# A hybrid mLSTM, attention and expert layer on one core: attention and routing moved into the expert loop

## What is computed

```python
h = modulate(rmsnorm(x, n1), sh1, sc1)
mq, mk, mv, mo, gt, aq, ak, av = split_cols(h @ w_in)
q = rmsnorm(aq.reshape(B, T, A_HEADS, A_DH), qg)          # 8 heads of 64, 2 key groups
m_out = mlstm_mixer(mq, mk, mv, mo, gt, ...)              # 4 heads of 128, both directions
a_out = attn_latent(rope_2d(q), rope_2d(k), v, kc, vc, sink)   # window of +-128 and 128 cached keys
x = x + g1 * (concat([m_out, a_out]) @ w_out)
h2 = modulate(rmsnorm(x, n2), sh2, sc2)

def peer(h, w_q, sub_a, sub_b, u_tab, v_tab):
    q = (x @ w_q).reshape(N, P_HEADS, P_DKEY)             # 8 heads, 2 halves of 128
    va, ia = lax.top_k(sa, 16); vb, ib = lax.top_k(sb, 16)    # sa, sb: q halves against 128 keys
    cand = va[..., :, None] + vb[..., None, :]
    top, pos = lax.top_k(cand, 16)                        # 8 x 16 = 128 experts per token
    gates = softmax(top)
    a = gelu(einsum('pd,phkd->phk', xb, u_tab[eb]))
    return einsum('phk,phkd->pd', gb * a, v_tab[eb])
x = x + g2 * peer(h2, ...)
```

## Time and profile before

| what | value |
|---|---|
| three runs, us | 4431.73, 6284.15, 4428.21 |
| median, us | 4431.73 |
| the profiled execution, us | 4423.65 |
| its span in the profile, us | 4421.8 |
| TensorE, busy share | 67% |
| VectorE, busy share | 54% |
| ScalarE, busy share | 19% |
| POOL, busy share | 36% |
| moved by DMA | 1348.41 MB, mean 305 GB/s |

### The profile page before, as it was taken

How to read it: one execution, slowest core, us unless ns; L and a number is a source line. 1 busy time by engine, 2 the same in 40 slices (tenths; PEclk the granted TensorE clock), 3 DMA queues, 4 the chain that set the end, 5 groups by cost and what they waited for, 6 DMA issues and landing times.

```text
span 4421.8 us, 41953 instructions
## 1 busy us (share of the span) xinstructions
PE 2957.5 (67%) x11157; PEld 1284.8 (29%) x11157; DVE 2402.1 (54%) x5728; ACT 826.1 (19%) x2523; POOL 1578.3 (36%) x1434
## 2 busy tenths in 40 slices
PE   8899778888863656656656655755755755755555
PEld 1444366555542212212312311311311411411111
DVE  1232354333316774674674684684684684685554
ACT  1111123323311111111111111111111111111111
POOL 0000011101102454454454454454554454455453
PEclk9899887777677878877877877877978977967777
DMA  9101133111134999999999999999999999999998
GB/s 368 56 34 41 59 101 114 39 43 47 38 130 189 418 415 390 420 409 389 420 404 391 420 408 391 420 404 391 416 408 402 409 395 408 409 404 406 403 420 368
DMA packets 220971, 1348.41 MB, mean 305 GB/s; under 512 B 23370, under 2 KB 34250, under 8 KB 71370
## 3 DMA queue, kind: packets, MB, share of 16 engines
q0 software_dynamic: 165888, 1208.03, 67.1%
q1 hardware_dynamic: 47212, 113.48, 7.4%
q10 hardware_dynamic: 7776, 25.96, 1.5%
HBM read 1316.04 MB, written 31.33 MB: 305 GB/s over the span
## 4 chain that ended last, share of the span: by engine, by line
DMA 37%; PE 12%; issue 10%; DVE 7%; POOL 3%; ACT 1%; POOLq 0%; SPq 0%; DVEq 0%; ACTq 0%
DMA pe_ring<-arg_uv,pe_fetch_idx 34%; PE pe_acc L1357 10%; POOL pe_ring L1311 3%; DMA pe_h<-h_scratch 2%; DVE pe_ring L1550 2%; PE pe_qP L1335 2%; ACT pe_diag L1423 1%; DVE pe_w L1555 1%; DMA pe_w_q<-arg_w_q 0%; DVE pe_rest L1514 0%; DVE pe_pos L1480 0%; DVE pe_ab L1517 0%; DVE pe_scores L1492 0%; DVE pe_rest L1511 0%; ACT pe_gelu L1418 0%
## 5 line engine op out<-in xcount | busy, mean ns | idle before, releaser
L1357 PE MATMUL pe_acc<-pe_ring,pe_diag 128*64 128x512 f32 x4608 | 1527.5, 799 | 1220.6 <-ACT pe_diag L1423 1220.6
L1311 POOL DMA_INDIRECT pe_ring<-arg_uv,pe_fetch_idx x1152 | 1391.4, 1208 | 1554.8 <-PE pe_acc L1357 1304.7
L1550 DVE CUSTOM_DVE_ANT_0 pe_ring<-pe_ring,pe_h 128x1024 f32<-128x1024 f32 x1152 | 1405.6, 1225 | 850.0 <-DMA pe_ring<-arg_uv,pe_fetch_idx 777.2
L1357 PEld LDWEIGHTS pe_acc<-pe_ring,pe_diag 128*64 128x64 f32 x4608 | 344.8, 167 | 2294.4 <-ACT pe_diag L1423 1809.4
L1418 ACT ACTIVATE pe_gelu<-pe_dot 128x2 f32<-128x2 f32 x576 | 117.1, 203 | 1876.9 <-DVE pe_dot L1550 1876.8
L1423 ACT ACTIVATE pe_diag<-pe_pick,pe_w 128x64 f32<-128x64 f32 x1152 | 337.9, 340 | 606.0 <-DVE pe_w L1555 606.0
L351 PE MATMUL in_z<-w_in,in_hT 128*128 128x512 f32 (+1 forms) x864 | 356.8, 576 | 22.3 <-ACT in_hT L381 22.3
L1335 PE MATMUL pe_qP<-pe_h2T,pe_w_q 128*128 128x128 f32 x2304 | 298.5, 285 | 29.3 <-DMA pe_w_q<-arg_w_q 29.3
L1335 PEld LDWEIGHTS pe_qP<-pe_h2T,pe_w_q 128*128 128x128 f32 x2304 | 273.8, 196 | 139.4 <-issue 139.4
L351 PEld LDWEIGHTS in_z<-w_in,in_hT 128*128 128x128 f32 x864 | 168.3, 196 | 205.7 <-issue 198.0
L1555 DVE TENSOR_TENSOR pe_w<-pe_gelu,gates 128x2 f32<-128x2 f32 x576 | 92.1, 160 | 189.0 <-ACT pe_gelu L1418 117.9
(11 more groups left out here) (256 smaller groups left out, 2418.4 us busy)
## 6 DMA issues: line engine op xcount, KB each, us to landing
ada_w<-arg_w_ada SPq DMA_DIRECT2D x12, 2048.0 KB, 10.3
pe_ring<-arg_uv,pe_fetch_idx POOLq DMA_INDIRECT x1152, 11.6
w_in<-arg_w_in SPq DMA_DIRECT2D x8, 1416.0 KB, 21.0
ml_qkT<-qkT_scratch SPq DMA_DIRECT2D x18, 512.0 KB, 3.5
pe_h<-h_scratch SPq DMA_DIRECT2D x36, 256.0 KB, 12.7
pe_w_q<-arg_w_q SPq DMA_DIRECT2D x8, 1024.0 KB, 12.9
ada_x<-arg_x ACTq DMA_DIRECT2D x9, 512.0 KB, 6.4
in_xn<-arg_x SPq DMA_DIRECT2D x9, 512.0 KB, 3.8
```

The costliest lines, as they stand in the source:

```text
L1311: pool.indirect_dma_start(out=ring[j][:], out_offset=None, in_=io.uv, in_offset=bass.IndirectOffsetOnAxis(ap=idg[half][:, j:j + 1], axis=0 ...
L1357: mm = pe.matmul(acc[b][cg * TOKS:(cg + 1) * TOKS, :], diag[:, j, :], ring[j][:, D + b * 512:D + (b + 1) * 512], start=False, stop=False)
L1550: dve.tensor_tensor_reduce(out=ring[j][:, 0:D], in0=ring[j][:, 0:D], in1=h2[i % NC][:], scale=1.0, scalar=0.0, op0=ALU.mult, op1=ALU.add, ...
```

## The change

`attend` and `peer` become one block, `mix_and_experts`. Attention (called the mixer) is cut into 19 steps per tile, routing into up to 44. One function, `drive`, lays out the order for every engine: the mixer of tile 0 alone; the routing of tile 0 with the mixers of tiles 1 and 2 beside it; then the expert loop, in which each of the first 128 pairs is followed by one routing step and one mixer step (114 mixer steps are left for them). Everything is written out straight, no loop is left. Scores, transposes and tails share two PSUM banks `ST`, so two heads are now done at a time: scores of both, then exp, transposes and values of both.

The pair itself. The gates no longer go through VectorE after the gelu; a block of eight selection matrices is filled with them ahead, and ScalarE scales it by the gelu:

```diff
-                        act.activation(gelu[:, sl], dot[:, sl], ACT.Gelu_apprx_tanh).then_inc(s_gelu, 1)
-                        act.wait_ge(s_w, n * NB + (q + 1))
-                            act.activation(diag[:, i % GROUP, :], pick[:], ACT.Copy, scale=w[:, i:i + 1]).then_inc(s_diag, 1)
+                    act.wait_ge(s_dot, (n + 1) * NC)
+                    act.activation(gelu[:, sl], dot[:, sl], ACT.Gelu_apprx_tanh).then_inc(s_gelu, 1)
+                    act.wait_ge(s_fill, n * NC // FILL + 1)
+                        last = act.activation(wsel[:, i, :], wsel[:, i, :], ACT.Copy, scale=gelu[:, i:i + 1])
-                        dve.tensor_tensor(w[:, sl], gelu[:, sl], g.gates[...], ALU.mult).then_inc(s_w, 1)
+                    if (r * NC) % FILL == 0:
+                        dve.tensor_tensor(wsel[:, lo:lo + FILL, :], pick[:]..., gates[t % 2][...], ALU.mult).then_inc(s_fill, 1)
-                        pool.tensor_copy(idg[half][:], g.eidx[:, t, ...])
-                    pe.matmul(acc[b][:], zero[:, 0:P], zero[:], start=True, stop=False)
```

w_q is streamed for the routing of tiles 0 to 2, in chunks of 128 columns (512 KB in runs of 512 B) into two buffers, and afterwards loaded whole, at pair 52 of tile 1:

```diff
+                def chunk(m):
+                    if m < NSIDE * STREAMED:
+                        if m >= WQ:
+                            sp.wait_ge(s_qd, m - WQ + 1)
+                        sp.dma_start(wq[m % WQ][:], src).then_inc(s_wq[m % WQ], 16)
```

At a tile's start SP now goes in this order, and loads h2T for the next routing only behind it:

```diff
+                def begin(t):
+                    ...
+                    if t:
+                        sp.wait_ge(s_out, t)
+                        sp.dma_start(io.y[t - 1], xo[:]).then_inc(s_st, 16)
+                        ...
+                        sp.wait_ge(s_st, t * 16)
+                    sp.wait_ge(s_x1o, t * 16 + 16)
+                    sp.dma_start(xo[:], g.x1_dram[t]).then_inc(s_xi, 16)
```

More of the change, by code:

```diff
@@ L1 @@
 from contextlib import ExitStack
-from itertools import chain, repeat
+from itertools import chain
 import numpy as np
@@ L651, in _ @@
                 step(0, True)
-                with pool.Fori(1, TILES) as t:
+                for t in range(1, TILES):
                     step(t)
@@ L1585, in _ @@
-                tile(0, 0)
-                with dve.Fori(1, TILES - 1) as t:
-                    tile(t, 1)
-                tile(TILES - 1, 1, more=False)
+                dve.wait_ge(s_const, 2)
+                dve.wait_ge(s_wo, 16 * KD)
+                dve.wait_ge(s_small, 96)
+                for k in range(KD // 2):
+                    last = dve.tensor_scalar(w_out[:, k, :], w_out[:, k, :], mhg[:, k:k + 1], None, ALU.mult)
+                last.then_inc(s_wom, 1)
+                drive(begin, pair, end, mixer, route)
```

1106 lines of the change are left out of this document (541 added, 565 removed).

## The result

The changed kernel takes 4474.1 us (median of four runs, 4468.7 to 4485.3), the one before 4431.7 beside it: a ratio of 1.010, with a 95% interval of 1.008 to 1.012. The ratios compare fast executions alone; one of the kernel before, 6284.15 us, was a slow one. That is slower, as forecast, but a third of the 2.9% that I gave, and it falls into the class "within 2%", to which I had given 0.24, not into "slower" with its 0.60. The interval also shows that a change of 1% can be told from none here, where I had said about 2%. The profiled execution has a span of 4476.3 us against 4421.8, so 54.5 us have to be found.

A forecast was written before the change was run, and what follows sets the result against it. The prediction took the expert stage as bound by its gathers, with DMA engines empty ahead of it. It summed 4421.8 - 359 + 448 + 21 + 28 = 4559.8, plus 1.9 outside the span, given as 4560 us; range 4360 to 4710.

The forecast's parts named there:

- within 2%: Whole kernel: outcome class for a time within 2% of the kernel before, chance 0.24.
- slower: Whole kernel: outcome class for a time over 4520 us, chance 0.60.
- The bound: Expert stage bound by its gathers, DMA engines empty in the stages ahead; engine order, not busy shares, decides whether overlap pays.
- Start of the gathers: Attention and routing before the expert loop: first gather at 1026 instead of 1384.9, 359 us earlier.
- The first two tiles: Expert tiles 0 and 1 with six mixers woven in: 1124 us against 675.9, 448 lost.
- the sum of a mixer's steps, 161 us: Expert tiles 0 and 1: one mixer tile's 19 steps cost 161 us, 8.5 per step.
- so the load is never hidden: ScalarE in the expert loop: each table load of about 1.3 us follows the wait for the dot, so counts in full.
- the mean, 2.65 us for every pair: TensorE in expert tiles 0 and 1: every pair costs 2.65 us, attention's matmuls run at a clock of 0.8.
- no part of a step lies beside another: Expert tiles 0 and 1: engines reach their mixer step through the same pair; a step with scores costs 11.65 us.
- attention is hidden after all: Rival for expert tiles 0 and 1: only the bytes count, 4204 us in all, chance 0.14.
- Tiles 2 to 8: Later expert tiles: pace unchanged, but query 0 waits for h2T's load, 4 us in each of seven tiles, 28.
- The chunk rival: Expert tiles 0 and 1: queries wait for w_q chunks landing in 26 us, 4690 us in all, chance 0.12.

The follow-up runs named there:

- e2: Against the changed kernel, all nine mixers run ahead of the expert loop, no mixer step in it: 4599.8 us, 1.039 to the kernel before.
- e3: Against the changed kernel, gelu replaced by a square that needs no table load of its own: 4453.9 us, 1.006 to the kernel before.
- e5: Against the changed kernel, w_q laid out by the host so chunks come in 4 KB runs: 4458.0 us, 1.007 to the kernel before.
- e1: Against the changed kernel, TensorE does its routing and mixer steps ahead of the pair: 4359.9 us, 0.985 to the kernel before.
- e9: Against the changed kernel, TensorE does only the mixer step ahead of the pair, queries stay behind: 4335.9 us, 0.979 to the kernel before.
- e4: Against the changed kernel, a mixer step behind every other pair of four tiles, w_q streamed for five: 4451.2 us, 1.006 to the kernel before.

## Why the prediction was right in direction and three times too large

**The bound.** Right: the DMA share in tiles 0 and 1 is 0.77 and not 1.00, engines have time free, and the order decides. The marks I had set for these tiles came: first gather at 1012 (forecast 1026), end of tile 1 at 2114 (2150), share 0.77 (0.7), 85 table loads (84 or more), clock 0.77 to 0.79 (0.8). VectorE's wait for scores came 20 times with 169 us, 8.5 each where I had said about 5. None of them could tell +1% from +3%, since the result is the small difference of two terms of 400 us. The measured time lies inside the range that I gave for all cases, 4360 to 4710, and just under the forecast's own, 4480 to 4640.

**Start of the gathers: -359, measured -374.** Two errors of the other sign. The block opened at 745.9 and not at 724: the stages ahead became 25 us longer, in `conditioning` 6, in `project_in` 13, in mLSTM 6, by their first loads in both traces. This I had put at zero and bounded by 15, and it was outside that bound. What the stores of the gates, the wider store of kv and the stores of h each take of it was not tried. From the block's opening to the first gather I had 302 us and it took 266: the stores of h2T stand at 837.9, 923.5 and 997.6, so the first mixer with its loads took 92 where I had 98, and those beside routing 86 and 74 us where I had 102 and 86. A mixer alone takes 65 us by e2 (392 over six) where I had 71, and with it some 20 of the 33 us of queries were exposed, where I had 31.

**The first two tiles: 1124 and 21, measured 1101.7.** The step that failed is the sum of a mixer's steps, 161 us. The trace has the start of every pair, and the time from one pair to the next is what the step between them cost. The table has the means for the steps without a query beside them (behind pairs 16 to 62 of tile 0 and 16 to 49 of tile 1, four or five of each kind):

| steps of a mixer | worked out | measured |
|---|---|---|
| 0 (scores) | 10.15 | 10.7 |
| 1, 3, 5, 7 (exps, transposes, values) | 6.7 each | 7.3, 7.5, 7.4, 7.7 |
| 2 and 6 (values, scores) | 11.65 each | 9.8, 9.5 |
| 4 (the same with the reciprocal) | 15.0 | 13.8 |
| 8 and 9 | 8.75 | 9.1 |
| 10 (turn) | 8.6 | 8.4 |
| 11 to 14 (w_out) | 36.7 | 36.5 |
| 15 and 16 (norm) | 8.3 | 7.8 |
| 17 and 18 (both ways of h2) | 17.8 | 18.6 |
| two more loads and the fill, booked apart | 5.9 | in the rows above |
| sum | 161 | 154.1 |

Six times the 7 us that are missing make 42, as much as the two tiles fell short. (The rest nearly cancels: queries, chunks and the end of tile 0 took 79 where I had 66 for the queries; the 14 pairs without a mixer, with the reload of w_q, 81 for 91; what stands before the first pair and behind the last 16 for 20.) Two of my premises were wrong in these rows.

The first is "so the load is never hidden". I had read the 30.5 us of waiting for dots before 25 loads as a wait ahead of each load. It is a single wait, ahead of the first one. The other 24 loads of the kernel before went out 0.02 us behind the instruction ahead of them, and behind 16 of them the gelu still waited 2.5 us or more for its dot, so they were hidden already:

```profile
1396.37 1.28 ACT L1418 ACT_TABLE_LOAD   x1 [30.50 <-DVE pe_dot L1550]
...
1637.58 1.28 ACT L1418 ACT_TABLE_LOAD   x1
1641.53 0.20 ACT L1418 ACTIVATE pe_gelu<-pe_dot 128x2 f32<-128x2 f32 x1 [2.66 <-DVE pe_dot L1550]
```

In the changed kernel's two tiles it is so for 16 of the 43 loads ahead of a gelu, among them all six behind the sigmoid's exp, which I had booked extra. Of the ten loads that I counted on a mixer's path, 77 us in all (9.2 a mixer or 55 us as the sum has them, since in an odd step it lets the pair run beside the first load), e3 confirms 24; by the steps without a query alone it is 5.5 us a mixer. The rule of the Trainium skill, page "ScalarE: Activation LUTs", section "What ACT_TABLE_LOAD costs", of a drain of 1.38 us beyond the load, is not seen here at all: exp starts 1.30 us after its load's start (1202.39 to 1203.69, as in the earlier trace rows), and less than a third of the load itself is paid.

The second is the mean, 2.65 us for every pair and a clock of 0.8 for the matmuls of attention. In these steps TensorE has one level or the other. In the odd steps the pair follows the wait of the even step and takes 3.65 us on average at the lower level, where I had 2.65; behind it TensorE works on almost without a break, transposes and values 2.7 us, and starts the next pair 1.05 later. With the square in e3 the odd steps are 1.0 shorter, 6.4 for 7.5: of their two loads, 2.6 us, only what reached beyond TensorE's work was paid. In steps 2 and 6 values and scores take 3.0 us where I had 4.3. Over two steps the errors partly cancel (17.1 for 18.35), which is luck.

The chunks, which I had put at nothing here and named as a rival, cost some 20 us beside the queries by e5 (79 us become 60).

**The premise that no part of a step lies beside another** held for the order that the change chose, and e1 and e9 show the price of that order: 149 and 140 us. In the odd steps ScalarE's work did lie beside TensorE's. My rival "attention is hidden after all" failed for the change, but a kernel with spaced steps, TensorE's mixer step ahead and long runs comes near it: 4261, for my 4204.

**Tiles 2 to 8: +28, measured +1.5.** The mechanism came, the price did not. The timeline of TensorE at the start of tile 2 in the changed kernel (answering to the earlier trace rows):

```profile
2128.40 3.47 PE L1275 MATMUL fx_acc<-fx_ring,fx_weighted_pick 128*64 128x512 f32 x8 [17.32 <-ACT fx_weighted_pick L1366]
2136.45 3.75 PE L1254 MATMUL rt_qP<-rt_h2T,rt_w_q 128*128 128x128 f32 x16 [4.58 <-issue]
2140.13 2.73 PE L1275 MATMUL fx_acc<-fx_ring,fx_weighted_pick 128*64 128x512 f32 x8
```

Query 0 now stands 4.6 us. Its row names no releaser, but the load of h2T went out at 2128.49 and landed, by the trace, at 2136.36, just ahead of it. The same wait of 4.5 to 5.2 us stands at the start of tiles 2 to 7; tile 8 has no queries, so "seven times" should have been six. But a tile takes 337.1 us as before (336.9): the lower bound that I had named, "nothing, if the ring's eight gathers cover it", is what holds. I had chosen 4 between 0 and 6 by the landing alone and had not asked what the DMA engines do in these 4 us; their share is 0.99 in the tile.

**The chunk rival** (26 us landing, 4690) had the right mechanism and the wrong place. In the first two tiles of the change they land in 8.8 us in the median (8.2 over all 48). Where steps are shorter TensorE waits for them more: 126 us in the two tiles of e2 and 46 in e4's first two, against 19.5. They kept both experiments from showing by their total what they were made for.

In sum: 15 us from the start, 42 from the two tiles and 26.5 from the seven, 84 of the 138 that I had forecast. The largest part is a mixer at 161 us where 154 were measured, the next the wait for h2T, which came and cost the tiles nothing.

## What to carry to other kernels

Where work is woven into a loop that is bound by transfers, its place decides: here it was nearly hidden when it stood ahead of the loop's own work on the engine that hands on to the others, with space between its steps. The same six attention tiles added 265 us in the change's order (1101.7 less 836.5; with long runs of w_q 316, 1077.7 less 761.5), and 40 to 60 spaced, ahead of the pair and with long runs. When two moved terms are large and of opposite sign, look at what each of them hides, and do the experiment that removes one entirely (e2): it found 162 us of chunks, of which the change's own waits showed 20. A weight that is streamed through two buffers costs by its landing as well as by its bytes: 75 of the 162 us went with the long runs, and some 61 are bytes. And a sum of waits in a table says nothing of how they are spread: look at single rows before you book one for every instruction.

## What the runs showed of the hardware that was not expected

- The same 512 KB land in 16.5 us in runs of 512 B and in 8.0 in runs of 4 KB, beside gathers, though their share of the DMA engines' time is 42 against 33 us a tile (with the other traffic of that queue).
- A table load is 1.283 us in every row, but one that stands ahead of its gelu's wait for the dots is hidden by that wait (the one at 1204.34, with 7.88 us of waiting behind it): 62 loads were worth 0.3 to 0.4 us each.
- TensorE's eight matmuls of a pair take 3.68 us at a granted clock of 0.50, the level of 1.2 GHz, after it had idled 5.1 us (1214.43), and 1.94 at 1.00, that of 2.4 GHz, after 0.95 us (1222.04). So a late handover costs the slower matmuls behind it as well. What it adds up to was not tried.
